# Attention of a hybrid layer: values mixed in column tiles, the query rotation on VectorE, keys and values ahead of the fourth scores product

## What is computed

```python
def _attend(q, k, v):
    def one(qi):
        s = jnp.einsum("bqhd,bkhd->bhqk", qi, k).astype(jnp.float32) * scale
        p = jax.nn.softmax(s, axis=-1).astype(v.dtype)
        return jnp.einsum("bhqk,bkhd->bqhd", p, v)

q = (_rmsnorm(q_lat, p["q_norm"]) @ p["w_uq"]).reshape(B, N, N_HEADS, QK_NOPE + QK_ROPE)
q_rope = _axial_rope(q_rope, tables)           # sample tokens alone
kv = (key_ckv @ p["w_ukv"]).reshape(B, M, N_HEADS, QK_NOPE + V_DIM)
o = _attend(q_full, k_full, v).reshape(B, N, N_HEADS * V_DIM) @ p["w_attn_proj"]
```

## Time and profile before

| what | value |
|---|---|
| median of 3 runs | 2763.88 us (2762.38 to 2764.07) |
| the profiled execution, its own time | 2761.58 us |
| its span in the trace | 2759.8 us |
| granted TensorE clock over the span | 0.994 |
| PE, PEld busy | 97%, 92% |
| DVE, ACT, POOL busy | 73%, 44%, 23% |
| attention of layer 0 | 594 us to 732 us of the span |
| attention of layer 1 | 1954 us to 2091 us, the same order |

### The profile page before, as it was taken

The page is one execution under the profiler, slowest core; times in us unless marked ns, Lnnn a source line. Parts: engine busy times, 40 slices in busy tenths (PEclk is TensorE's granted clock), DMA queues, the critical chain, the costliest instruction groups (busy, mean ns, idle before and its releaser), DMA issues. The chain is left out here.

```text
span 2759.8 us, 44748 instructions
## 1 busy us (share of the span) xinstructions
PE 2689.4 (97%) x17878; PEld 2536.0 (92%) x17878; DVE 2017.3 (73%) x2736; ACT 1216.1 (44%) x1998; POOL 622.6 (23%) x323
## 2 busy tenths in 40 slices
PE   6999999999999999999999999999999999999997
PEld 3999999977799999999989999999778999999997
DVE  6878878766534788887888879787664358776876
ACT  5533435556422543343564335355563236443433
POOL 1322422022100124232321413210220002242230
PEclk9999999999999999999999999999999999999999
DMA  6445432210121253423224444322101222212312
GB/s 239 152 147 161 146 123 68 72 56 26 43 84 63 92 168 116 130 99 109 93 101 152 139 159 145 102 75 67 46 27 64 74 65 85 92 63 84 105 49 77
DMA packets 86446, 273.02 MB, mean 99 GB/s; under 512 B 8736, under 2 KB 10016, under 8 KB 86112
## 3 DMA queue, kind: packets, MB, share of 16 engines
q1 hardware_dynamic: 84800, 265.60, 29.1%
q10 hardware_dynamic: 1440, 4.56, 0.5%
HBM read 267.21 MB, written 2.92 MB: 98 GB/s over the span
## 5 line engine op out<-in xcount | busy, mean ns | idle before, releaser
L624 POOL TENSOR_TENSOR sums_raw<-raw_pairs 128x1024 f32<-128x1024 f32 x88 | 238.3, 2708 | 1627.9 <-DVE weights_lo L1706 1050.2
L652 PE MATMUL ps<-h_hi,weights_hi 128*128 128x322 f32 (+1 forms) x1408 | 440.3, 313 | 8.6 <-DVE t_lo L1706 3.1
L656 PE MATMUL ps<-h_hi,weights_lo 128*128 128x322 f32 (+1 forms) x1408 | 437.4, 311 | 0.0
L654 PE MATMUL ps<-h_lo,weights_hi 128*128 128x322 f32 (+1 forms) x1408 | 436.8, 310 | 0.0
L1706 DVE TENSOR_TENSOR weights_lo<-sums_raw,weights_hi 128x1024 fp32r<-128x1024 f32 (+2 forms) x296 | 329.7, 1114 | 56.5 <-ACT weights_hi L1237 26.7
L652 PE MATMUL ps<-t_hi,weights_hi 128*128 128x322 f32 (+1 forms) x1056 | 332.2, 315 | 5.3 <-DVE h_lo L1706 5.3
L652 PE MATMUL ps<-a_hi,weights_hi 128*128 128x320 f32 x1408 | 325.1, 312 | 3.3 <-DVE tmp L1884 2.5
L656 PE MATMUL ps<-t_hi,weights_lo 128*128 128x322 f32 (+1 forms) x1056 | 327.5, 310 | 0.0
L654 PE MATMUL ps<-t_lo,weights_hi 128*128 128x322 f32 (+1 forms) x1056 | 326.4, 309 | 0.0
L654 PE MATMUL ps<-a_lo,weights_hi 128*128 128x320 f32 x1408 | 321.5, 309 | 0.0
L656 PE MATMUL ps<-a_hi,weights_lo 128*128 128x320 f32 x1408 | 321.5, 309 | 0.0
(11 more groups left out here) (273 smaller groups left out, 5680.6 us busy)
## 6 DMA issues: line engine op xcount, KB each, us to landing
raw_pairs<-in_w_up SPq DMA_DIRECT2D x87, 1024.0 KB, 4.9
wm<-in_w_mod SPq DMA_DIRECT2D x88, 512.0 KB, 3.9
raw<-in_w_merge SPq DMA_DIRECT2D x32, 704.0 KB, 4.0
sums_raw<-in_w_down SPq DMA_DIRECT2D x56, 384.0 KB, 3.2
wm<-in_w_mod SPq DMA_DIRECT2D x80, 256.0 KB, 3.0
sums_raw<-in_w_down SPq DMA_DIRECT2D x64, 320.0 KB, 3.0
raw<-in_w_in SPq DMA_DIRECT2D x16, 512.0 KB, 3.6
raw<-in_w_out SPq DMA_DIRECT2D x16, 512.0 KB, 3.5
```

The costliest lines, as they stand in the source:

```text
L624: nc.gpsimd.tensor_tensor(sums_raw[:, UNIT:3 * UNIT].rearrange("p (s c) -> p s c", s=2), w.rearrange("p (s c) -> p s c", s=2)[:, :, 0:UNIT ...
L652: nc.tensor.matmul(out, whi, v, start=first, stop=False)
L654: nc.tensor.matmul(out, whi, v, start=False, stop=False)
L656: mm = nc.tensor.matmul(out, wlo, v, start=False, stop=last)
```

## The change

Six things.

- `values(j)` no longer uses a 128-column stationary operand over 512 columns. The 64 columns of values are multiplied twice, as two column tiles of 128x64, each over 256 query columns, into partitions 0 to 63 and 64 to 127 of bank 7. The sums come from four column tiles of 128x32 of ones, each over 128 query columns. For block 6 there is one 64-wide tile of values and one of ones over 128 columns. All goes to bank 7.
- `o_copy` goes from ACT. `o_norm` now runs after every head on DVE, and reads PSUM: two reciprocals (128x128 and 64x128), eight products of 32x128 and one of 64x128. Its `s_o32` is what `values(0)` of the next head waits for; `scores(1)` no longer waits for it.
- The rotation of heads 1 to 7 moves from POOL to DVE, in front of `weight_lo`. Head 0 stays on POOL.
- On PE `keys_values` moves in front of `scores(3)`; on ACT `split_queries` and `keys` move in front of `exponent(3)`.
- Two DVE memsets per layer, which wrote the ones beside the values, go.
- POOL's `weight_sums(44)` waits in addition until DVE has split the last activation tile of pair 43 (`s_alo`).

```diff
@@ POOL, weight_sums and the loop
                     pool.wait_ge(s_lo34, pair)
+                    if pair == 2 * PAIRS:
+                        pool.wait_ge(s_alo, pair + START)
...
-                for h in range(HEADS):
-                    rotate(l * HEADS + h)
+                rotate(l * HEADS)
@@ PE, scores
-                    if j == 1:
-                        pe.wait_ge(s_o32, hd)
-                        if h == 0:
-                            pe.wait_ge(s_frlo, (l + 1) * 3)
+                    if j == 1 and h == 0:
+                        pe.wait_ge(s_frlo, (l + 1) * 3)
@@ PE, values
-                    out, v_in = (bank(7), ex[j % 2]) if j < 6 else (bank(1 if following else 3, 0, P), ex[j % 2][:, 0:P])
-                    nc.tensor.matmul(out, vals[b][:, j, :], v_in, start=j in (0, 6), stop=j in (5, 6)).then_inc(s_pv, 1)
+                    v = vals[b][:, j, b * VD:(b + 1) * VD]
+                    if j < 6:
+                        for n in range(2):
+                            nc.tensor.matmul(bank(7, 0, S2)[n * VD:(n + 1) * VD], v, ex[j % 2][:, n * S2:(n + 1) * S2],
+                                             start=j == 0, stop=False)
+                        for n in range(4):
+                            mm = nc.tensor.matmul(bank(7, S2, S2 + P)[32 * n:32 * n + 32], ones[:, 0:32],
+                                                  ex[j % 2][:, n * P:(n + 1) * P], start=False, stop=j == 5)
+                    else:
+                        nc.tensor.matmul(bank(7, S2 + P, S2 + 2 * P)[0:VD], v, ex[j % 2][:, 0:P], start=True, stop=True)
+                        mm = nc.tensor.matmul(bank(7, S2 + P, S2 + 2 * P)[VD:P], ones[:, 0:VD], ex[j % 2][:, 0:P],
+                                              start=True, stop=True)
+                    mm.then_inc(s_pv, 1)
@@ PE, attend
-                scores(3)
                 if following:
                     pe.wait_ge(s_rowc, hd + 1)
                     keys_values(c1 % 2)
+                scores(3)
@@ ACT, attend (o_copy and its calls go)
-                exponent(3)
                 if following:
                     split_queries(hd + 1)
                     keys(hd + 1, mixp, head_chunk(h + 1))
+                exponent(3)
+                if following:
                     values_copy(hd + 1)
...
-                if h == HEADS - 2:
-                    maximum_copy(hd + 1)
-                o_copy(hd)
-                if h < HEADS - 2:
                     maximum_copy(hd + 1)
@@ DVE, mixer_step
-                for s in range(2):
-                    c = (1 - s) * VD
-                    nc.vector.memset(vals[s][:, :, c:c + VD], 1.0)
...
                 for h in range(HEADS):
-                    if h and h % 2 == 0:
-                        o_norm(l, h // 2 - 1)
+                    if h + 1 < HEADS:
+                        rotate(hd0 + h + 1)
                     weight_lo(c0 + HEADS_C + h + 2)
...
-                o_norm(l, OT - 1)
+                    o_norm(hd0 + h)
@@ DVE, o_norm
+            def o_norm(hd):
+
+                rows0 = hd % 2 * VD
+                dve.wait_ge(s_pv, (hd + 1) * 7)
+                nc.vector.reciprocal(sums_inv[:, 0:P], bank(7, S2, S2 + P))
+                nc.vector.reciprocal(sums_inv[VD:P, P:2 * P], bank(7, S2 + P, S2 + 2 * P)[VD:P]).then_inc(s_rinv, 1)
+                dve.wait_ge(s_rinv, hd + 1)
+                for n in range(4):
+                    for r in range(0, VD, 32):
+                        tt(o32[rows0 + r:rows0 + r + 32, TOK[n]:TOK[n] + P],
+                           bank(7, n % 2 * P, (n % 2 + 1) * P)[n // 2 * VD + r:n // 2 * VD + r + 32],
+                           sums_inv[32 * n:32 * n + 32, 0:P], ALU.mult)
+                tt(pro(o32[rows0:rows0 + VD]), bank(7, S2 + P, S2 + 2 * P)[0:VD], sums_inv[VD:P, P:2 * P],
+                   ALU.mult).then_inc(s_o32, 1)
```

More of the change, by code:

```diff
@@ L344, in build @@
         vt = tmp[:, 2 * SAMPLE + 2 * T:2 * SAMPLE + 2 * T + KEYS]
-        sums = acc
+        sums_inv = acc[:, 0:2 * P]
         mod_acc = [tmp[:, g * D:(g + 1) * D] for g in range(2)]
@@ L440, in build @@
         s_st, s_exp, s_pv = sem("scores_ready"), sem("exp_ready"), sem("values_mixed")
-        s_o32, s_rinv, s_on = sem("o_copied"), sem("row_inverse"), sem("o_normed")
+        s_o32, s_rinv = sem("o_normed"), sem("row_inverse")
         s_ohi, s_olo = sem("o_hi_ready"), sem("o_ready")
@@ L1582, in maximum_copy @@
                 nc.scalar.activation(q_hi[hd % 2][QK:QK + 2, :], ps[0:2, 5 * 512:5 * 512 + T], ACT.Copy).then_inc(s_rowc, 1)
[L1584 to L1592, removed]
             def o_hi(l, t):
-                act.wait_ge(s_on, l * OT + t + 1)
+                act.wait_ge(s_o32, (l * OT + t + 1) * 2)
                 nc.scalar.activation(ot_hi[:, t, :], o32[:], ACT.Copy).then_inc(s_ohi, 1)
@@ L2208, in maximum_lo, with rotate, o_lo @@
                 lo_of(nm2[:, :, 1], nmx[:], nm2[:, :, 0]).then_inc(s_nmlo, 1)
-            def o_norm(l, t):
-                dve.wait_ge(s_o32, (l * OT + t + 1) * 2)
[L2212 to L2219, removed]
+            def rotate(hd):
+                dve.wait_ge(s_q32, hd + 1)
+                tt(rot[NOPE:QK], q32[QK:P], rope_tab[QK:P, :], ALU.mult).then_inc(s_rot, 1)
+                dve.wait_ge(s_rot, hd * 3 + 1 + START)
+                tt(q32[NOPE:QK], q32[NOPE:QK], rope_tab[NOPE:QK, :], ALU.mult).then_inc(s_rot, 1)
+                dve.wait_ge(s_rot, hd * 3 + 2 + START)
+                tt(q32[NOPE:QK], q32[NOPE:QK], rot[NOPE:QK], ALU.add).then_inc(s_rot, 1)
+            def o_norm(hd):
[11 more added lines that the diff above has]
+                   ALU.mult).then_inc(s_o32, 1)
+            def o_lo(l, t):
+                dve.wait_ge(s_o32, (l * OT + t + 1) * 2)
                 dve.wait_ge(s_ohi, l * OT + t + 1)
```

## The result

| | before | after |
|---|---|---|
| median, runs beside each other | 2763.98 us (4 runs) | 2809.8 us (4 runs) |
| ratio | | 1.0167, 95% interval 1.0149 to 1.0184 |
| span of the profiled execution | 2759.8 us | 2807.7 us |
| granted TensorE clock over the span | 0.994 | 0.987 |

The changed kernel is slower by 45.8 us. The forecast was +19.4 with a range up to 2800, so the sign was right and the time was outside. The last row of the table is the first hint: the granted clock is lower, and no term of the forecast touched it.

A forecast was written before the change was run, and what follows sets the result against it. PE's own work was taken to bound the kernel, busy 97% of the span. Terms 18.2 + 4.0 - 1.6 - 1.2 = +19.4 us on the median of 2763.88 gave 2783 us, range 2762 to 2800.

The forecast's parts named there:

- block `v1` to `v4`, each: PE's value products 1 to 4 of a head: each block holds PE 1.12 us instead of 0.87, +0.25 us.
- `v0` / `v5` and `v6`: First and last value products of a head on PE: +0.1 us for the first, +0.2 for the last two.
- 14 heads: Heads 0 to 6 of both layers: +1.3 us each from the value products, +18.2 us in all.
- last heads at full clock: Last head of each layer: late o_norm, value products and the way out of tiles, +2.0 us, twice, +4.0.
- gains: Memsets dropped ahead of head 0's maximum, -1.6 us; POOL's sums of pair 44 moved later, -1.2 us.
- The price of a block: Value products on PE: 0.64 us array time, 0.34 in and out of tiles, 0.13 inner change of tile width.
- The two rivals with free changes: Value products: inner tile change free, 2769 us, chance 0.20; all tile changes free, 2739 us, faster, chance 0.14.
- maximum_rows follows without a wait as now: End of a head on PE: no wait behind `v6`, so `v5` and `v6` take 1.28 us instead of 1.07.
- The cover is 0.6 us: Heads before the last: o_norm takes 3.7 to 4.0 us, ending at 706.4, before the next `v0` at 707.0.
- I had this as a rival: o_norm late in every head: 1.6 us over, 1.0 beyond cover, +1.0 x 16, 2799 us, chance 0.09.
- the sum for the last head: Last head: o_norm's lateness +0.5, `v0` +0.1, `v1` to `v4` +1.0, way out of tiles +0.4: +2.0 us.
- Edits at nothing: Rotation on DVE, o_copy off ACT, and the move of keys_values and keys: no gain and no cost.

The follow-up runs named there:

- e10_split: The kernel before, with each value product written as two column tiles of 128x64 over the same 512 columns, nothing else: 2794.9 us, ratio 1.0112.
- e3_one_width: The kernel after, with sums of blocks 0 to 5 from two 64-wide tiles of ones instead of four 32-wide; result not the reference's: 2783.7 us.
- e4_small_edits: The kernel before, with only the rotation on DVE, the keys_values reorder and POOL's later sums(44); no tiles, memsets kept: 2764.7 us, ratio 1.0003.
- e5_stall2176: The kernel before, with an extra ACT copy of 32x2176 ahead of o_copy of head 6 in both layers: 2770.5 us, ratio 1.0024.
- e13_stall_half: The kernel before, with an extra ACT copy of 32x1100 ahead of o_copy of head 6 in both layers: 2767.3 us, ratio 1.0012.
- e11_last_width: The kernel after, with the last head's sums from two 64-wide tiles instead of four 32-wide ones; result not the reference's: 2795.3 us.

## Where the prediction was right and where it failed

| term, both layers | forecast | measured |
|---|---|---|
| block `v1` to `v4`, each | +0.25 | +0.27 |
| `v0` / `v5` and `v6` | +0.1 / +0.2 | +0.1 / +0.35 |
| o_norm ahead of `v0` | 0 | +0.2 to 0.3 |
| 14 heads | 14 x 1.3 = 18.2 | 14 x 1.7 = 23.7 |
| last heads at full clock | 2 x 2.0 = 4.0 | 2 x 3.1 = 6.2 |
| half clock, last heads and gate_f | 0 | 2 x 8.5 = 17.0 |
| gains | -2.8 | seen in their places, not in the total |
| sum | +19.4 | 46.9 by the marks, 45.8 by the medians |

*The price of a block held.* All its parts did: tiles side by side, 0.34 for in and out (e10_split), 0.13 for the inner change (0.14, e3_one_width). The two rivals with free changes fell with them (in the first, 0.9 x 16 is 14.4, not 14.2), and with them the way in which the kernel could have been faster.

*"maximum_rows follows without a wait as now" failed.* I took that from the earlier trace rows, where it follows a 128-wide product. Behind the 64-wide tiles of `v6` its load waits too. That is the 0.15 in `v5` and `v6`:

```profile
711.49 0.14 PEld L1114 LDWEIGHTS ps<-tmp,v 128*64 128x64 f32 x1
...
711.80 0.26 PEld L1070 LDWEIGHTS ps<-ident_r,nm 128*2 128x2 f32 x5 [0.17 <-issue]
```

*"The cover is 0.6 us" failed by its price.* The reciprocal was scaled from 320 to 128 columns as if it had no fixed part: 0.84 forecast, 0.96 measured. A product of 32x128 was put at 0.2 and takes 0.30, against 0.49 for 322 columns. With 4.7 us instead of 3.9 the cover of 0.6 was used up and 0.2 to 0.3 were left, in every head. I had this as a rival, with the missing fixed part named as its cause, at 1.6 us over; it was half of that. The missing fixed part is seen in the products, which read PSUM in both rows; for the reciprocal it is not shown alone, since the row of 320 columns reads SBUF and those of 128 read PSUM. That DVE hears of `v6` 0.2 us after its end stood in the forecast without a row; the first reciprocal starts 0.12 us behind maximum_rows (711.92 and 711.80), where the forecast had 0.29. The same 0.8 explains most of the last head at full clock: `v0` came 4.9 us behind maximum_rows (before 3.7), so +1.2, not +0.5.

*The step that made the prediction wrong is the sum for the last head.* It counted o_norm's lateness at its own length, +0.5 us, and all work behind it at full clock. The gap was in the rows: PE had 0.78 and 0.59 us of idle time at that place, and the change made the second one longer. What it does to the clock was 17.0 of the 26.4 us by which the forecast was short. Nothing in the trace of before showed the clock fall at this place, but no term, bound or rival asked what happens if the gap grows, and the range had no room for it.

*Edits at nothing.* In the changed kernel they were: all heads take the same 19.6 to 19.8 us. e4_small_edits shows that the rotation on DVE is not free behind a pair's o_norm. It also shows that it costs DVE less than its own 2.5 us: without POOL's rotation beside them other operations of DVE are shorter, the product over 128x640 takes 0.82 us instead of 1.57, the low part over 128x1408 1.62 instead of 2.98. Seven rotations are 17 us, and DVE's busy time in the attention of layer 0 rose from 80.1 to 87.9.

*Gains.* Each was there where it was said to be. The second was given back in part one pair later, and none shows in the total: the stages outside of attention differed by up to 5 us between the profiled kernels, also where nothing in them was changed.

## What to carry to other kernels

Count a column tile by its changes of shape, and not by its columns alone: here 0.34 us for each excursion from 128-wide products and 0.14 for each change between tile widths, against 0.23 us of array time that the tiles saved. Before an edit makes a wait of TensorE longer, look at the granted clock around it: here two microseconds of idle time cost 8.5 more behind them, and a few matmuls that nobody reads, put into the wait, bring it all back. When a duration is scaled down, take two rows of different size, since the fixed part decides for small operations.

## What the runs showed of the hardware

- After a gap the clock fell to 1.2 GHz, and how long it stayed there depended on the work that followed: 3.4 us with 128-wide products (e5_stall2176 in both layers, e13_stall_half in one); 3.4 us in four layers and 6.8 in one where the tiles were 64 wide (e10_split, e11_last_width, e3_one_width); 20.5 us in both layers with four 32-wide tiles per block (the kernel after). I had expected one length for all.
- At the edge it is not settled by the code alone: with equal gaps in both layers, one layer kept its clock and the other did not (e13_stall_half, gaps of 0.78 and 1.71 us, last heads of 13.2 and 14.8 us; e10_split, 0.78 and 0.58 us with tiles, 15.6 and 14.0 us).
- Reciprocals of 128x128 and 64x128 from PSUM both take 0.96 us: half the partitions saved nothing.
- DVE's product over 128x640 in SBUF took 0.82 us once POOL no longer rotated in the heads, against 1.57 before (e4_small_edits and the kernel before); the reciprocals over 128x320 took 2.1 in both.
